# Attention in pairs of heads: scores in the two row halves of TensorE's array, values in its two column halves

## The chip, the cores and the metric

The kernel runs on one core of a Trainium2 chip. The metric is the time of one execution in microseconds (us), measured on the device. Lower is better. The engines are TensorE (PE in the rows, its weight loads PEld), VectorE (DVE), ScalarE (ACT), GpSimd (POOL) and SyncE (SP), whose queue issues most transfers.

## What is computed

One decoder layer over 256 tokens of width 1024. The change touches two parts of its first sub-layer: causal attention with 8 heads of 64 (one block of 256 keys, so every head is plain causal softmax with a distance bias), and a gated linear recurrence (HGRN2) with 4 heads of 128, in chunks of 64 tokens. Cut from the reference:

```
s_own = (jnp.einsum('bhqd,bhkd->bhqk', qc, k_own).astype(F32)
         - slopes[None, :, None, None] * dist_own[None, None])
s_own = jnp.where(dist_own[None, None] >= 0, s_own, -jnp.inf)
...
probs = jax.nn.softmax(scores, axis=-1).astype(v.dtype)
...
a = jnp.einsum('bhntd,bhnsd->bhnts', qh * jnp.exp(b - b_ref), kh * jnp.exp(b_ref - b))
ds = jnp.einsum('bhnsd,bhnsv->nbhdv', kh * jnp.exp(b_last - b), vh)
...
mixed = (jax.nn.sigmoid(ga) * (ya @ w_branch_a[l])
         + jax.nn.sigmoid(gb) * (yb @ w_branch_b[l]))
```

Behind it come the output projection, a layer norm, and the PEER part: 16384 experts, all of which are multiplied densely, in a U stage and a V stage that take most of the time.

## The kernel before

All large weights run through PE in pieces of 128x1024 in a ring of four (`raw`, `w_hi`, `w_lo`): SP loads piece m into `raw` when the low part of piece m-4 is made, ACT copies it to `w_hi`, DVE makes `w_lo` (`split_lo`, L1318), and PE multiplies high and low parts in three matmuls (L931 to L933). Two pieces make a block b; the blocks 8 to 33 hold the input projections, branch projections, output projection and query projection. Every block is 48 matmuls of 256 columns. Each engine has one program written out by hand in order of the blocks, and each step waits for semaphores.

Attention and HGRN are fp32 and lie between the blocks. On PE they are in `after(b)`, behind block b. A head h passes through it in four blocks: its products (L1101, L1102: queries of rows 0 to 127 with 128 keys, then queries 128 to 255 with 256 keys, both with 64 contracted rows into bank `px[0]`) behind block 11+h; DVE adds the distance bias and takes the maximum (L1402 to L1406) at the head of its block 13+h, ahead of the two `split_lo` of that block; ACT takes the exponentials (L754), DVE normalises (L1475 to L1477); three transposes (L1110, into `px[1]`) behind block 12+h; ACT copies them to `pT` in its block 14+h; values (L1119, L1120, into one 64-row half of bank `px[2]`) behind block 13+h. One half of the array in rows or in columns is used at a time. DVE and ACT run up to two blocks ahead of PE, so that their "block 13+h" lies beside PE's block 11+h or 12+h.

HGRN's steps are in the same function: `aT` in block 12, the transposes of `k_l` in 13, the state matmuls (L1078) in 14 and 15, the outputs (L1089, L1092) in 17, the transposes of `o_nat` (L1131) in 19. They use three banks: `pv[0]`, `pv[1]`, `px[3]`.

Of the kernel before, what the change touches and what calls it, by code (L numbers as in the profile page):

```python
# [5 lines left out]
P = 128  # L6
# [4 lines left out]
ALU = mybir.AluOpType  # L11
# [3 lines left out]
T = 256  # L15
# [3 lines left out]
HEADS = 8  # L19
# [89 lines left out]
def layer(nc, xT_d, x_d, c_d, ada1_d, ada3_d, w_ada_d, b_cols_d, b_ada_d, w1_d, ws_d, lb_d, norm_g_d, ln1_g_d, ln1_b_d, ln1_cols_d,  # L109
          keys_d, u_d, v_d, u_rows_d, ln2_g_d, ln2_b_d, x1_d, gates_d, out_d):  # L110
    with ExitStack() as ctx:
# [88 lines left out]
        pT = sb("pT", AR + 16640, [3 * P])  # L200
# [185 lines left out]
        def _(sp):  # L386
# [52 lines left out]
            for b in range(FIRST + 2, NA):  # L439
# [3 lines left out]
                if b == BRANCH + 2:  # L443
                    sp.wait_ge(pv_done, HEADS)
# [182 lines left out]
        def _(act):  # L627
# [67 lines left out]
            for b in range(FIRST + 2, NA):  # L695
# [33 lines left out]
                if b == 14:  # L729

                    for t, src in enumerate((px[3], pv[0])):
# [8 lines left out]
                if b == 15:  # L740
                    for t, src in enumerate((pv[1], px[3])):
                        act.wait_ge(kl_done, t + 1)
                        copy(kl_nat[:, t], src[:, :].rearrange("p (h t) -> p h t", h=HG)).then_inc(kl_ready, 1)
                if b == 19:
                    for t, src in enumerate((px[3], pv[0])):
# [30 lines left out]
                if b == 21:  # L776

                    for t, src in enumerate((pv[1], px[3])):
# [148 lines left out]
        def _(pe):  # L927
# [122 lines left out]
            def after(b):  # L1050

                if b == 12:
                    pe.wait_ge(qk_ready, 1)
                    pe.wait_ge(act_took, evac_count(QA + 1))
                    for t, dst in enumerate((px[3], pv[0])):
# [25 lines left out]
                if b == 17:  # L1081
                    pe.wait_ge(aT_ready, 1)
                    pe.wait_ge(state_ready, 3)
                    for t, dst in enumerate((px[3], pv[0])):
# [10 lines left out]
                h = b - 11  # L1095
                if 0 <= h < HEADS:
                    pe.wait_ge(act_took, evac_count(KA + 1))
                    if h >= 1:
                        pe.wait_ge(s_max, h)
                    r = slice((h % 2) * DH, (h % 2 + 1) * DH)  # L1100
                    nc.tensor.matmul(px[0][:, 0:P], qT[r, h // 2, 0:P], kT[r, h // 2, 0:P], start=True, stop=True)  # L1101
                    nc.tensor.matmul(px[0][:, P:3 * P], qT[r, h // 2, P:T], kT[r, h // 2, :], start=True, stop=True) \  # L1102
                        .then_inc(s_done, 1)

                def transposes(h):
                    pe.wait_ge(p_ready, h + 1)
                    if h >= 1:
                        pe.wait_ge(pT_ready, h)
# [859 lines left out]
```

## Time and profile before

| | |
|---|---|
| median of 3 runs | 984.92 us (984.75 to 985.06) |
| the profiled execution, its time | 984.99 us |
| its span (first to last instruction) | 983.2 us |
| mean granted clock of TensorE | 0.997 of 2.4 GHz |
| PE busy | 967.6 us, 98% |
| DVE, ACT, POOL busy | 794.3, 511.9, 373.7 us |
| transfers over the span | 239.56 MB, mean 244 GB/s |

Attention and HGRN lie between 83.7 and 163.5 us. In rows of the timeline the columns are the start in us, the duration in us, engine, line, operation, output and inputs, shape, and how many of the same kind were merged. Ends of matmuls are modelled, so the distance between starts tells what one costs. "128*64" is the part of the array that is used, rows by columns. A matmul in fp32 leaves two records, a transpose one.

### The profile page before, as it was taken

What the parts mean: (1) busy time and instruction counts of PE and PEld (TensorE: products, weight loads), DVE (VectorE), ACT (ScalarE), POOL (GpSimd) and SP (SyncE); (2) the same over time, 40 slices, a digit from 0 to 9 for tenths busy, and PEclk for the clock granted to TensorE, in tenths of its full rate; (3) what the DMA queues carried; (4) which work ended last, traced back from release to release, by engine and by line L of the source; (5) the groups of instructions that cost most, each with busy time, mean ns of one, the idle gap of its engine ahead of it and who ended that gap; (6) DMA issues with size and microseconds to landing.
All of it is one profiled execution on the core that took longest, in us unless ns stands there. A gap on an engine that the chain in (4) does not pass through costs nothing.

```text
span 983.2 us, 17773 instructions
## 1 busy us (share of the span) xinstructions
PE 967.6 (98%) x6823; PEld 894.3 (91%) x6823; DVE 794.3 (81%) x1538; ACT 511.9 (52%) x737; POOL 373.7 (38%) x234
## 2 busy tenths in 40 slices
PE   8999999999999999999999999999999999999996
PEld 8999889999999999999999999888888888888884
DVE  6979888894887989887688888787875878987866
ACT  5477656655445464546444444544445444445542
POOL 1010101001888787777887774122231222100002
PEclk9999999999999999999999999999999999999998
DMA  9987958985656787886766666788879989986661
GB/s 354 412 301 278 335 164 303 326 259 215 194 193 180 195 205 173 218 198 184 175 166 158 151 172 200 253 300 290 301 266 387 311 304 329 339 286 221 214 193 43
DMA packets 86659, 239.56 MB, mean 244 GB/s; under 512 B 26928, under 2 KB 27952, under 8 KB 84912
## 3 DMA queue, kind: packets, MB, share of 16 engines
q1 hardware_dynamic: 59536, 207.94, 62.3%
q0 software_dynamic: 26752, 30.49, 13.5%
q8 instruction: 54, 0.88, 0.4%
q14 instruction: 29, 0.24, 0.1%
q10 hardware_dynamic: 288, 0.01, 0.0%
HBM read 227.84 MB, written 10.55 MB: 242 GB/s over the span
## 4 chain that ended last, share of the span: by engine, by line
PE 91%; DVE 4%; DMA 2%; ACT 1%; SPq 1%; POOL 1%; issue 0%; POOLq 0%; ACTq 0%; DVEq 0%
PE px L1256 35%; PE pw L931 16%; PE pw L932 16%; PE pw L933 15%; PE px L1231 3%; DMA raw<-in_w 2%; DVE w_lo L1318 1%; PE pv L933 1%; PE pv L932 1%; PE pv L931 1%; PE px L931 1%; PE px L932 1%; PE px L933 1%; PE px L1188 0%; PE px L1119 0%
## 5 line engine op out<-in xcount | busy, mean ns | idle before, releaser
L629 ACT ACTIVATE w_hi<-raw 128x1024 fp32r<-128x1024 f32 x308 | 324.8, 1058 | 295.7 <-PE px L1256 157.9
L1318 DVE TENSOR_TENSOR w_lo<-raw,w_hi 128x1024 fp32r<-128x1024 f32 x285 | 347.2, 1226 | 96.3 <-ACT w_hi L629 94.8
L931 PE MATMUL pw<-a_hi,w_hi 128*128 128x240 f32 (+1 forms) x1248 | 348.1, 279 | 0.3 <-DVE a_lo L1568 0.3
L932 PE MATMUL pw<-a_lo,w_hi 128*128 128x240 f32 (+1 forms) x1248 | 344.2, 276 | 0.0
L933 PE MATMUL pw<-a_hi,w_lo 128*128 128x240 f32 (+1 forms) x1248 | 344.2, 276 | 0.0
L582 POOL DMA_INDIRECT gates_spill<-gate,place x128 | 231.9, 1812 | 65.9 <-issue 44.0
L931 PEld LDWEIGHTS pw<-a_hi,w_hi 128*128 128x128 f32 x1248 | 236.4, 189 | 2.3 <-issue 1.2
L932 PEld LDWEIGHTS pw<-a_lo,w_hi 128*128 128x128 f32 x1248 | 236.4, 189 | 0.0
L933 PEld LDWEIGHTS pw<-a_hi,w_lo 128*128 128x128 f32 x1248 | 236.4, 189 | 0.0
L1256 PE MATMUL px<-w_hi,ws_lo 128*128 128x512 f32 x512 | 159.0, 389 | 0.0
L1256 PE MATMUL px<-w_lo,ws_hi 128*128 128x512 f32 x512 | 158.9, 389 | 0.0
L1256 PE MATMUL px<-w_hi,ws_hi 128*128 128x512 f32 x512 | 158.8, 389 | 0.0
L1256 PEld LDWEIGHTS px<-w_hi,ws_lo 128*128 128x128 f32 x512 | 96.1, 188 | 20.0
L1256 PEld LDWEIGHTS px<-w_lo,ws_hi 128*128 128x128 f32 x512 | 96.1, 188 | 19.9
L1256 PEld LDWEIGHTS px<-w_hi,ws_hi 128*128 128x128 f32 x512 | 96.1, 188 | 19.8
L881 ACT ACTIVATE W<-pw 128x480 f32<-128x480 f32 (+11 forms) x64 | 34.3, 536 | 99.2 <-PE pw L933 99.1
L587 POOL DMA_INDIRECT sp_row<-in_v,sp_idx x16 | 28.6, 1790 | 99.3 <-DVE sp_acc L1851 81.2
L545 POOL DMA_DIRECT2D gates_spill<-zero x16 | 11.8, 737 | 140.2 <-DVE w_lo L1318 140.2
L587 POOL DMA_INDIRECT sp_row<-in_u_rows,sp_idx x16 | 28.4, 1776 | 90.7 <-DVE sp_w L1837 86.5
L512 POOL TENSOR_TENSOR w_lo<-raw,w_hi 128x1024 fp32r<-128x1024 f32 x22 | 52.4, 2403 | 20.9 <-ACT w_hi L629 20.9
L1799 DVE TENSOR_TENSOR ws_lo<-W,ws_hi 128x240 fp32r<-128x240 f32 x128 | 51.2, 402 | 0.0
L629 ACT ACTIVATE ws_hi<-W 128x240 fp32r<-128x240 f32 x128 | 49.3, 387 | 1.2 <-DVE W L1792 1.2
(382 smaller groups left out, 1239.3 us busy)
## 6 DMA issues: line engine op xcount, KB each, us to landing
raw<-in_u SPq DMA_DIRECT2D x128, 512.0 KB, 4.3
raw<-in_v SPq DMA_DIRECT2D x128, 512.0 KB, 4.3
raw<-in_ws SPq DMA_DIRECT2D x52, 512.0 KB, 6.7
ada<-in_ada SPq DMA_DIRECT2D x20, 512.0 KB, 6.9
ada<-in_w_ada SPq DMA_DIRECT2D x16, 512.0 KB, 7.4
gates_spill<-zero POOLq DMA_DIRECT2D x16, 512.0 KB, 7.6
g_row<-gates_spill SPq DMA_DIRECT2D x32, 256.0 KB, 5.1
raw<-in_w SPq DMA_DIRECT2D x7, 1024.0 KB, 11.8
```

The costliest lines, as they stand in the source:

```text
L512: nc.gpsimd.tensor_tensor(w_lo[:, m % RING], raw[:, m % RING], w_hi[:, m % RING].bitcast(F32), ALU.subtract) \
L582: nc.gpsimd.indirect_dma_start(gates_d, bass.IndirectOffsetOnAxis(ap=place[:, h, k:k + 1], axis=0), gate[0][:, h, k:k + 1], None, compute_ ...
L587: nc.gpsimd.indirect_dma_start(sp_row[x % 2][:, :], None, table, bass.IndirectOffsetOnAxis(ap=sp_idx[:, x % NS:x % NS + 1], axis=0)).then_ ...
L629: return nc.scalar.activation(out, in_, ACT.Copy, **kw)
L881: last = nc.scalar.activation(W[:, 2 * g:2 * g + 2, 0:left], src[:, :, 0:left], ACT.Gelu)
L931: nc.tensor.matmul(out, lh, rh, start=start and x == 0, stop=False)
L932: nc.tensor.matmul(out, lh, rl, start=False, stop=False)
L933: last = nc.tensor.matmul(out, ll, rh, start=False, stop=stop and x == len(pairs) - 1)
L1231: last = nc.tensor.matmul(px[n % 4][:, y * P:(y + 1) * P], oh_i[n % 2][:, y], oh_j[n % 2][:, y], start=True, stop=True)
L1256: last = nc.tensor.matmul(px[2 * t + half][:, :], l[:, v % RING, q], r[:, half * 512:(half + 1) * 512], start=v == 0 and x == 0, stop=v == ...
L1318: v.tensor_tensor(w_lo[:, m % RING], raw[:, m % RING], w_hi[:, m % RING].bitcast(F32), ALU.subtract).then_inc(lo_ready, 1)
L1799: v.tensor_tensor(ws_lo[:, r % RING, 0:TD], W[:, r], ws_hi[:, r % RING, 0:TD].bitcast(F32), ALU.subtract).then_inc(wsplit_lo, 1)
```

## The change

Heads go in pairs j = 0 to 3. Products: the two heads of a pair alternate between the row halves of the array and write to `px[0]` and `px[1]`. Transposes: six, into `px[2]` and `px[3]`. Values: three rounds of 128 columns, in each of which the two heads alternate between the column halves, written into the last quarter of `px[2]` and `px[3]`. Products and the transposes of the pair before stand behind the odd blocks 11 to 19, values behind the even blocks 14 to 20. DVE and ACT treat a pair at once, in odd blocks; DVE's bias and maximum of pair j now wait for the transposes of pair j-1. HGRN gives up `px[3]` and uses `pv[0]` and `pv[1]`; the state matmuls of chunks 0 and 1 stand behind block 14 and those of chunk 2 behind block 15, where they wait for DVE's first copy of the state.

```diff
         prob = sb("prob", AR + 15872, [2, 3 * P])
-        pT = sb("pT", AR + 16640, [3 * P])
+        pT = sb("pT", AR + 16640, [2, 3 * P])
...
-    h = b - 13
-    if 0 <= h < HEADS:
-        act.wait_ge(s_max, h + 1)
-        x = h % 2
-        for t, q in enumerate((slice(0, P), slice(P, 3 * P))):
-            last = nc.scalar.activation(prob[:, x, q], prob[:, x, q], ACT.Exp,
-                                        bias=rmax[:, 2 * x + t:2 * x + t + 1],
-                                        accum_out=rsum[:, 2 * x + t:2 * x + t + 1])
+    j = (b - 13) // 2
+    if b % 2 and 0 <= j < HEADS // 2:
+        act.wait_ge(s_max, j + 1)
+        for x in range(2):
+            for t, q in enumerate((slice(0, P), slice(P, 3 * P))):
+                last = nc.scalar.activation(prob[:, x, q], prob[:, x, q], ACT.Exp,
+                                            bias=rmax[:, 2 * x + t:2 * x + t + 1],
+                                            accum_out=rsum[:, 2 * x + t:2 * x + t + 1])
         last.then_inc(p_exp, 1)
-    h = b - 14
-    if 0 <= h < HEADS:
-        act.wait_ge(pT_done, h + 1)
-        if h >= 1:
-            act.wait_ge(pv_done, h)
-        copy(pT[:, :], px[1][:, 0:3 * P]).then_inc(pT_ready, 1)
+    j = (b - 15) // 2
+    if b % 2 and 0 <= j < HEADS // 2:
+        act.wait_ge(pT_done, j + 1)
+        if j >= 1:
+            act.wait_ge(pv_done, j)
+        for x in range(2):
+            last = copy(pT[:, x], px[2 + x][:, 0:3 * P])
+        last.then_inc(pT_ready, 1)
...
-    for h in range(1, HEADS, 2):
-        if b == h + 15:
-            act.wait_ge(pv_done, h + 1)
-            copy(yaT[:, h // 2], px[2][:, 0:T]).then_inc(ya_copied, 1)
+    j = (b - 16) // 2
+    if b % 2 == 0 and 0 <= j < HEADS // 2:
+        act.wait_ge(pv_done, j + 1)
+        for t in range(TT):
+            last = copy(yaT[:, j, t * P:(t + 1) * P], px[2 + t][:, 3 * P:4 * P])
+        last.then_inc(ya_copied, 1)
...
     if b == 13:
         pe.wait_ge(qk_ready, 2)
-        for t, dst in enumerate((pv[1], px[3])):
-            if t:
-                pe.wait_ge(aT_copied, 1)
+        for t, dst in enumerate((pv[1], pv[0])):
+            pe.wait_ge(aT_copied, t + 1)
...
     if b in (14, 15):
-        for n in ((0,) if b == 14 else (1, 2)):
-            dst = (pv[0], pv[1], px[3])[n]
-            pe.wait_ge(kl_ready, n // 2 + 1)
-            pe.wait_ge(aT_copied, 2)
-            if n:
-                pe.wait_ge(kl_ready, 2)
+        for n in ((0, 1) if b == 14 else (2,)):
+            dst = pv[n % 2]
+            pe.wait_ge(kl_ready, 2)
+            if n == 2:
+                pe.wait_ge(state_ready, 1)
             t, q = n // 2, slice((n % 2) * CH, (n % 2 + 1) * CH)
             for h in range(HG):
...
-    h = b - 11
-    if 0 <= h < HEADS:
+    def products(j):
         pe.wait_ge(act_took, evac_count(KA + 1))
-        if h >= 1:
-            pe.wait_ge(s_max, h)
-        r = slice((h % 2) * DH, (h % 2 + 1) * DH)
-        nc.tensor.matmul(px[0][:, 0:P], qT[r, h // 2, 0:P], kT[r, h // 2, 0:P], start=True, stop=True)
-        nc.tensor.matmul(px[0][:, P:3 * P], qT[r, h // 2, P:T], kT[r, h // 2, :], start=True, stop=True) \
-            .then_inc(s_done, 1)
...
-    def transposes(h):
-        pe.wait_ge(p_ready, h + 1)
-        if h >= 1:
-            pe.wait_ge(pT_ready, h)
-        for x in range(3):
-            last = nc.tensor.transpose(px[1][:, x * P:(x + 1) * P], prob[:, h % 2, x * P:(x + 1) * P], ident[:, :])
+        if j >= 1:
+            pe.wait_ge(s_max, j)
+        for q, k, o in ((slice(0, P), slice(0, P), slice(0, P)), (slice(P, T), slice(0, T), slice(P, 3 * P))):
+            for x in range(2):
+                r = slice(x * DH, (x + 1) * DH)
+                last = nc.tensor.matmul(px[x][:, o], qT[r, j, q], kT[r, j, k], start=True, stop=True)
+        last.then_inc(s_done, 1)
...
+    def transposes(j):
+        pe.wait_ge(p_ready, j + 1)
+        if j >= 1:
+            pe.wait_ge(pT_ready, j)
+            pe.wait_ge(ya_copied, j)
+        for x in range(2):
+            for y in range(3):
+                q = slice(y * P, (y + 1) * P)
+                last = nc.tensor.transpose(px[2 + x][:, q], prob[:, x, q], ident[:, :])
         last.then_inc(pT_done, 1)
-    def values(h):
-        pe.wait_ge(pT_ready, h + 1)
+    def values(j):
+        pe.wait_ge(pT_ready, j + 1)
         pe.wait_ge(act_took, evac_count(VA + 1))
-        if h >= 2 and h % 2 == 0:
-            pe.wait_ge(ya_copied, h // 2)
-        o, v = slice((h % 2) * DH, (h % 2 + 1) * DH), slice(h * DH, (h + 1) * DH)
-        nc.tensor.matmul(px[2][o, 0:T], va[:, 0, v], pT[:, 0:T], start=True, stop=False)
-        nc.tensor.matmul(px[2][o, P:T], va[:, 1, v], pT[:, T:3 * P], start=False, stop=True).then_inc(pv_done, 1)
...
-    if 0 <= b - 12 < HEADS:
-        transposes(b - 12)
-    if 0 <= b - 13 < HEADS:
-        values(b - 13)
+        for t, a, y in ((0, 0, 0), (1, 0, 1), (1, 1, 2)):
+            for x in range(2):
+                v = slice((2 * j + x) * DH, (2 * j + x + 1) * DH)
+                last = nc.tensor.matmul(px[2 + t][x * DH:(x + 1) * DH, 3 * P:4 * P], va[:, a, v],
+                                        pT[:, x, y * P:(y + 1) * P], start=a == 0, stop=a == t)
+        last.then_inc(pv_done, 1)
...
+    j = (b - 11) // 2
+    if b % 2 and 0 <= j < HEADS // 2:
+        products(j)
+    if b % 2 and 1 <= j <= HEADS // 2:
+        transposes(j - 1)
+    j = (b - 14) // 2
+    if b % 2 == 0 and 0 <= j < HEADS // 2:
+        values(j)
...
-    h = b - 13
-    if 0 <= h < HEADS:
-        x = h % 2
-        dve.wait_ge(s_done, h + 1)
-        if h == 0:
+    j = (b - 13) // 2
+    if b % 2 and 0 <= j < HEADS // 2:
+        dve.wait_ge(s_done, j + 1)
+        if j == 0:
             dve.wait_ge(consts, 3)
-        if h >= 2:
-            dve.wait_ge(pT_done, h - 1)
-        link(v.scalar_tensor_tensor(prob[:, x], dist[:, :], -(2.0 ** (-8.0 * (h + 1) / HEADS)), px[0][:, 0:3 * P],
-                                    ALU.mult, ALU.add))
-        v.reduce_max(rmax[:, 2 * x:2 * x + 1], prob[:, x, 0:P], AX)
-        link(v.reduce_max(rmax[:, 2 * x + 1:2 * x + 2], prob[:, x, P:3 * P], AX))
-        mark(v.tensor_scalar(rmax[:, 2 * x:2 * x + 2], rmax[:, 2 * x:2 * x + 2], -1.0, None, ALU.mult), s_max, h + 1)
+        else:
+            dve.wait_ge(pT_done, j)
+        for x in range(2):
+            ins = v.scalar_tensor_tensor(prob[:, x], dist[:, :], -(2.0 ** (-8.0 * (2 * j + x + 1) / HEADS)),
+                                         px[x][:, 0:3 * P], ALU.mult, ALU.add)
+        link(ins)
+        top = rmax[:, 0:4].rearrange("p (x t) -> p x t", t=2)
+        v.reduce_max(top[:, :, 0], prob[:, :, 0:P], AX)
+        link(v.reduce_max(top[:, :, 1], prob[:, :, P:3 * P], AX))
+        mark(v.tensor_scalar(rmax[:, 0:4], rmax[:, 0:4], -1.0, None, ALU.mult), s_max, j + 1)
...
-    h = b - 13
...
-        dve.wait_ge(p_exp, h + 1)
-        link(v.reciprocal(rinv[:, 2 * x:2 * x + 2], rsum[:, 2 * x:2 * x + 2]))
-        v.tensor_scalar(prob[:, x, 0:P], prob[:, x, 0:P], rinv[:, 2 * x:2 * x + 1], None, ALU.mult)
-        v.tensor_scalar(prob[:, x, P:3 * P], prob[:, x, P:3 * P], rinv[:, 2 * x + 1:2 * x + 2], None,
-                        ALU.mult).then_inc(p_ready, 1)
+    j = (b - 13) // 2
+    if b % 2 and 0 <= j < HEADS // 2:
+        dve.wait_ge(p_exp, j + 1)
+        link(v.reciprocal(rinv[:, 0:4], rsum[:, 0:4]))
+        for x in range(2):
+            for t, q in enumerate((slice(0, P), slice(P, 3 * P))):
+                ins = v.tensor_scalar(prob[:, x, q], prob[:, x, q], rinv[:, 2 * x + t:2 * x + t + 1], None, ALU.mult)
+        ins.then_inc(p_ready, 1)
```

PE, in the order of the program, all that stands between block 15 and block 16 and between block 16 and block 17 (the rows of the blocks themselves, L931 to L933, lie between the `px2` row with `pT` and the next `px0` row). Before:

```order
L1078 MATMUL pv<-vh_113,kl_nat_106 128x128 [waits kl_ready,aT_copied]
L1078 MATMUL pv<-vh_113,kl_nat_106 128x128 x3
L1078 MATMUL px3<-vh_113,kl_nat_106 128x128 [waits kl_ready,aT_copied]
L1078 MATMUL px3<-vh_113,kl_nat_106 128x128 x3
L1101 MATMUL px0<-kT_118,qT_117 128x128 [waits s_max,act_took]
L1102 MATMUL px0<-kT_118,qT_117 128x256
L1110 MATMUL px1<-ident_54,prob_120 128x128 [waits pT_ready,p_ready]
L1110 MATMUL px1<-ident_54,prob_120 128x128 x2
L1119 MATMUL px2<-pT_121,va_119 64x256 [waits ya_copied,act_took,pT_ready]
L1120 MATMUL px2<-pT_121,va_119 64x128
```

Behind block 16 stood the same without the four rows of L1078. After the change, behind block 15:

```order
L1080 MATMUL pv<-vh_113,kl_nat_106 128x128 [waits state_ready,kl_ready]
L1080 MATMUL pv<-vh_113,kl_nat_106 128x128 x3
L1104 MATMUL px0<-kT_118,qT_117 128x128 [waits s_max,act_took]
L1104 MATMUL px1<-kT_118,qT_117 128x128
L1104 MATMUL px0<-kT_118,qT_117 128x256
L1104 MATMUL px1<-kT_118,qT_117 128x256
L1115 MATMUL px2<-ident_54,prob_120 128x128 [waits ya_copied,pT_ready,p_ready]
L1115 MATMUL px2<-ident_54,prob_120 128x128 x2
L1115 MATMUL px3<-ident_54,prob_120 128x128 x3
L1124 MATMUL px2<-pT_121,va_119 64x128 [waits act_took,pT_ready]
L1124 MATMUL px2<-pT_121,va_119 64x128
L1124 MATMUL px3<-pT_121,va_119 64x128 x4
```

The last three rows stand behind block 16, where nothing else is left. Products and transposes are gone from there, and the second head's products have moved up into the row half beside the first head's.

DVE at its block 17, the head of the block to the normalising. Before:

```order
L1402 SCALAR_TENSOR_TENSOR prob_120<-dist_122,px0 128x384 [waits pT_done,s_done]
L1404 TENSOR_REDUCE rmax_72<-prob_120 128x1 [waits dve_chain]
L1405 TENSOR_REDUCE rmax_72<-prob_120 128x1
L1406 TENSOR_SCALAR rmax_72<-rmax_72 128x2 [waits dve_chain]
L1318 TENSOR_TENSOR w_lo_51<-raw_49,w_hi_50 128x1024 [waits hi_ready,s_max]
L1318 TENSOR_TENSOR w_lo_51<-raw_49,w_hi_50 128x1024 [waits hi_ready]
L1459 TENSOR_TENSOR state_116<-state_116,decay_71 128x512 [waits ds_done]
```

After the change:

```order
L1412 SCALAR_TENSOR_TENSOR prob_120<-dist_122,px0 128x384 [waits pT_done,s_done]
L1412 SCALAR_TENSOR_TENSOR prob_120<-dist_122,px1 128x384
L1416 TENSOR_REDUCE rmax_72<-prob_120 128x2 [waits dve_chain]
L1417 TENSOR_REDUCE rmax_72<-prob_120 128x2
L1418 TENSOR_SCALAR rmax_72<-rmax_72 128x4 [waits dve_chain]
L1328 TENSOR_TENSOR w_lo_51<-raw_49,w_hi_50 128x1024 [waits hi_ready,s_max]
L1328 TENSOR_TENSOR w_lo_51<-raw_49,w_hi_50 128x1024 [waits hi_ready]
L1471 TENSOR_TENSOR state_116<-state_116,decay_71 128x512 [waits ds_done]
```

The first row's wait for `pT_done` was for the transposes of two heads back, and is for those of the pair just before now; the two `w_lo` rows stand behind twice the work. In block 18 the first five rows are missing on DVE.

## Rows read from the trace of the kernel before

**Rows 1.** Page, part 1: busy us, share of the span, instructions of each engine.

```profile
PE 967.6 (98%) x6823; PEld 894.3 (91%) x6823; DVE 794.3 (81%) x1538; ACT 511.9 (52%) x737; POOL 373.7 (38%) x234
```

**Rows 2.** Waits of PE from 60 to 175 us: total, times, longest.

```profile
PE px L1110 <- DVE prob L1477: 0.2, 1, 0.2
```

**Rows 3.** Windows: length, busy by engine, clock, share of transfer engines, GB/s.

```profile
80.00:100.00 20.00, 20.00 (x162) 19.08 (x162) 19.72 (x29) 14.78 (x26) 1.42 (x2) 1.00 0.90 315
...
165.00:180.00 15.00, 15.00 (x127) 15.00 (x126) 13.29 (x17) 10.48 (x10) 1.50 (x2) 1.00 1.03 408
200.00:210.00 10.00, 10.00 (x86) 10.00 (x85) 9.83 (x16) 5.08 (x6) 0.71 (x1) 1.00 0.81 281
```

**Rows 4.** Timeline of PE behind block 13: products, transposes, values, dense again.

```profile
100.39 0.49 PE L1101 MATMUL px<-kT,qT 64*128 64x128 f32 x2
...
101.24 0.55 PE L1110 MATMUL px<-ident,prob 128*128 128x128 f32 x3
101.72 0.65 PE L1119 MATMUL px<-pT,va 128*64 128x256 f32 x2
...
102.51 0.39 PE L931 MATMUL pw<-a_hi,w_hi 128*128 128x256 f32 x1
```

**Rows 5.** Timeline of PE behind block 12: transposes, then dense.

```profile
93.29 0.55 PE L1110 MATMUL px<-ident,prob 128*128 128x128 f32 x3
93.60 0.36 PE L931 MATMUL pw<-w_hi,a_hi 128*128 128x256 f32 x1
```

**Rows 6.** Timeline of PE, block 20: first and last matmul, then block 21's first.

```profile
156.79 0.36 PE L931 MATMUL pw<-a_hi,w_hi 128*128 128x256 f32 x1
...
162.51 0.28 PE L933 MATMUL pw<-a_hi,w_lo 128*128 128x256 f32 x1
...
163.51 0.39 PE L931 MATMUL pw<-a_hi,w_hi 128*128 128x256 f32 x1
```

**Rows 7.** PE at the PEER scores: timeline, and the window of L1188 alone.

```profile
247.34 1.16 PE L1188 MATMUL px<-keys,qpT 64*128 64x128 f32 x16
248.43 0.38 PE L931 MATMUL pw<-a_hi,w_hi 128*128 128x240 f32 x1
...
247.30:247.36 0.06, 0.02 (x2) 1.00 0.83 341
```

**Rows 8.** Timeline of PE in HGRN's outputs, two of seven like steps.

```profile
136.44 0.44 PE L1089 MATMUL pv<-vh,aT 128*64 128x128 f32 x4
136.66 0.44 PE L1092 MATMUL pv<-state,q_x 128*64 128x128 f32 x4
```

**Rows 9.** Timeline of PE behind block 15: 16 records of L1078, then the products.

```profile
117.07 0.82 PE L1078 MATMUL pv<-vh,kl_nat 64*128 64x128 f32 x5
...
118.61 0.27 PE L1101 MATMUL px<-kT,qT 64*128 64x128 f32 x1
```

**Rows 10.** Timeline of DVE in its blocks 19 and 20.

```profile
139.24 0.56 DVE L1402 SCALAR_TENSOR_TENSOR prob<-dist,px 128x384 f32<-128x384 f32 x1 [3.23 <-PE px L1102]
...
140.68 2.36 DVE L1318 TENSOR_TENSOR w_lo<-raw,w_hi 128x1024 fp32r<-128x1024 f32 x2
...
145.61 0.16 DVE L1475 RECIPROCAL rinv<-rsum 128x2 f32<-128x2 f32 x1
...
146.27 0.20 DVE L1484 RECIPROCAL rms_i<-rms 128x8 f32<-128x8 f32 x1
...
150.16 0.55 DVE L1402 SCALAR_TENSOR_TENSOR prob<-dist,px 128x384 f32<-128x384 f32 x1
...
151.59 2.36 DVE L1318 TENSOR_TENSOR w_lo<-raw,w_hi 128x1024 fp32r<-128x1024 f32 x2
```

**Rows 11.** Timeline of ACT for one head: exponentials, then two copies.

```profile
130.46 0.40 ACT L754 ACTIVATE prob<-prob,rmax 128x128 f32<-128x128 f32 x1 [2.19 <-DVE rmax L1406]
...
131.36 0.47 ACT L629 ACTIVATE pT<-px 128x384 f32<-128x384 f32 x1
131.73 0.37 ACT L629 ACTIVATE yaT<-px 128x256 f32<-128x256 f32 x1
```

More of the change, by code:

```diff
@@ L443, in _ @@
                 if b == BRANCH + 2:
-                    sp.wait_ge(pv_done, HEADS)
+                    sp.wait_ge(pv_done, HEADS // 2)
                     sp.dma_start(x_nat[:, :, :], x_d.rearrange("(a p) n -> p a n", p=P)).then_inc(x_landed, 16)
@@ L729, in _ @@
                 if b == 14:
-                    for t, src in enumerate((px[3], pv[0])):
+                    for t, src in enumerate((pv[1], pv[0])):
                         act.wait_ge(aT_done, t + 1)
@@ L740, in _ @@
                 if b == 15:
-                    for t, src in enumerate((pv[1], px[3])):
+                    for t, src in enumerate((pv[1], pv[0])):
                         act.wait_ge(kl_done, t + 1)
@@ L744, in _ @@
                 if b == 19:
-                    for t, src in enumerate((px[3], pv[0])):
+                    for t, src in enumerate((pv[1], pv[0])):
                         act.wait_ge(o_done, t + 1)
                         copy(o_nat[:, t], src[:, :]).then_inc(o_copied, 1)
-                h = b - 13
-                if 0 <= h < HEADS:
-                    act.wait_ge(s_max, h + 1)
-                    x = h % 2
-                    for t, q in enumerate((slice(0, P), slice(P, 3 * P))):
-                        last = nc.scalar.activation(prob[:, x, q], prob[:, x, q], ACT.Exp,
-                                                    bias=rmax[:, 2 * x + t:2 * x + t + 1],
-                                                    accum_out=rsum[:, 2 * x + t:2 * x + t + 1])
-                    last.then_inc(p_exp, 1)
-                h = b - 14
-                if 0 <= h < HEADS:
-                    act.wait_ge(pT_done, h + 1)
-                    if h >= 1:
-                        act.wait_ge(pv_done, h)
-                    copy(pT[:, :], px[1][:, 0:3 * P]).then_inc(pT_ready, 1)
+                j = (b - 13) // 2
[6 more added lines that the diff above has]
+                                                        accum_out=rsum[:, 2 * x + t:2 * x + t + 1])
+                    last.then_inc(p_exp, 1)
+                j = (b - 15) // 2
[6 more added lines that the diff above has]
+                    last.then_inc(pT_ready, 1)
                 if b == 19:
@@ L776, in _ @@
                 if b == 21:
-                    for t, src in enumerate((pv[1], px[3])):
+                    for t, src in enumerate((pv[1], pv[0])):
                         act.wait_ge(ybT_done, t + 1)
@@ L1054, in after @@
                     pe.wait_ge(act_took, evac_count(QA + 1))
-                    for t, dst in enumerate((px[3], pv[0])):
+                    for t, dst in enumerate((pv[1], pv[0])):
                         for h in range(HG):
@@ L1061, in after @@
                     pe.wait_ge(qk_ready, 2)
-                    for t, dst in enumerate((pv[1], px[3])):
-                        if t:
-                            pe.wait_ge(aT_copied, 1)
+                    for t, dst in enumerate((pv[1], pv[0])):
+                        pe.wait_ge(aT_copied, t + 1)
                         for h in range(HG):
@@ L1083, in after @@
                     pe.wait_ge(state_ready, 3)
-                    for t, dst in enumerate((px[3], pv[0])):
+                    for t, dst in enumerate((pv[1], pv[0])):
                         for h in range(HG):
@@ L1126, in after @@
+                    last.then_inc(pv_done, 1)
[7 more added lines that the diff above has]
+                    values(j)
                 if b == 19:
                     pe.wait_ge(yb_ready, 1)
-                    for t, dst in enumerate((pv[1], px[3])):
+                    for t, dst in enumerate((pv[1], pv[0])):
@@ L1135, in after @@
                     pe.wait_ge(gt1_ready, 2)
-                    pe.wait_ge(pT_ready, HEADS)
+                    pe.wait_ge(pT_ready, HEADS // 2)
                     for half in range(2):
@@ L1453, in _ @@
                         dve.wait_ge(ds_done, n + 1)
-                        src = (pv[0], pv[1], px[3])[n]
+                        src = pv[n % 2]
                         if n == 0:
@@ L1491, in _ @@
                     dve.wait_ge(act_hi, 1)
-                    for t, src in enumerate((pv[1], px[3])):
+                    for t, src in enumerate((pv[1], pv[0])):
                         q = slice(t * P, (t + 1) * P)
```

2 lines of the change are left out of this document (removed).

## The prediction

> **What bounds the kernel now.** I read the page's busy times first: TensorE (PE) is busy for 967.6 us of the 983.2 us span [rows 1]. Then the waits of PE between 60 and 175 us, the stretch in which this code runs: one wait, 0.2 us [rows 2]. So every matmul taken out of this stretch moves all that follows, as long as VectorE (DVE), ScalarE (ACT) and the transfers still deliver before PE asks. That condition is not empty: DVE is busy for 19.72 of the 20 us from 80 to 100, and for 9.83 of 10 from 200 to 210; the transfers fill 1.03 of their engines from 165 to 180 [rows 3]. The reader is to see two things: a PE without holes, and a DVE that is nearly as full.
>
> Then PE's timeline after weight block 13, for the price of each step of a head by the distance between starts [rows 4]: products 0.85 (100.39 to 101.24), three transposes 0.48 when values follow, values 0.79 (101.72 to 102.51). Where dense work follows the transposes, they take 0.31 [rows 5]. A whole block is 5.72 from its first to its last matmul, and values alone put 1.00 between the last matmul and the next dense one, where 0.12 would stand without them: net 0.88 [rows 6].
>
> **The change part by part.**
>
> *Attention on PE.* Now: 8 products, 6.80; transposes seven times 0.48 and once 0.31, 3.67; values seven times 0.79 and once 0.88, 6.41. Sum 16.88.
>
> Afterwards four pairs. Do two heads in the two row halves run at once? The profile of before has that pattern: the PEER scores L1188 alternate row halves and banks. Their 16 records take 1.09 from the first to the next dense matmul, and two of them start in the first 0.06 us [rows 7]. One half alone needs 0.11 for a record, so 16 in a row would take 1.76 and two streams of eight 0.88; 1.09 is two streams and 0.2 for the change of shape, which the 0.85 of one head contains as well. A pair of products is thus 0.85. For the column halves the HGRN outputs L1089 and L1092 serve: alternating halves of one bank, four records in 0.22 (136.44 to 136.66), 0.055 each [rows 8]. The values of a pair are 12 records of 128 columns, 0.66, the same as the two records of 256 and two of 128 that one head costs now; so 0.79, or 0.88 alone in a block. Transposes: no overlap, six take 0.31 and three more at 0.11, 0.64.
>
> Sum: products 3.40; transposes 2.56; values three times alone, 2.64, and once behind state matmuls, 0.79 and up to 0.15 for changing from row to column halves, 0.94. Together 9.54. Taken out: 7.3.
>
> *Smaller items.* The one wait of PE, 0.2, stands before head 7's transposes; their normalised probabilities are ready a block earlier now: gain 0.2. HGRN's 28 output matmuls and 16 transposes only change banks: nothing. The state matmuls: where one set follows another in the other row half they overlap at the seam, 16 records in 1.54 instead of 1.76 [rows 9]. Before there are two such seams (n=0 against head 3's products, n=1 against n=2), afterwards one: loss 0.2. From aT to dense no shape changes in block 12 any more: gain 0.1. So 7.3 + 0.2 - 0.2 + 0.1 = 7.4.
>
> *ACT and DVE.* The work shrinks: three Exp/Sigmoid/Sqrt table loads fewer on ACT, some fixed costs on DVE. What counts is that it comes in lumps, in odd blocks only, and that DVE has a new wait at the head of the lump: pT_done(j), the transposes of the pair before (until now one head back in the other half of `prob`, long done). Behind it in DVE's queue stand the two w_lo splits of the block, on which PE and SP's next loads of raw wait. The lump's size: one head's maximum takes 1.43 (150.16 to 151.59) [rows 10]. Two take at most 2.86; merged, with two drains fewer, I take 2.3.
>
> Two places decide. D is the first dense matmul after the transposes of the pair before.
>
> (a) Values in blocks 16 and 18 need pT. The last transpose ends 0.2 after D (93.29 + 0.55 against 93.60) [rows 5]: DVE starts at D + 0.2, ends at D + 2.5 (at most 3.1); ACT's exponentials take 0.90 a head (130.46 to 131.36), 1.80 for two; the copies 0.37 and 0.47 [rows 11]. pT at D + 5.1, at most 5.7. PE asks at 5.72 + 0.12, D + 5.85. No wait, with 0.15 to 0.7 in hand. The two splits behind the maximum are ready by D + 5.5, the first is wanted at D + 6.7.
>
> (b) Block 19, counted from the first matmul D of block 18. DVE: maximum until D + 2.5; splits, squares and their sum as now, 140.68 to 145.61, 4.93; normalising 0.66 a head (145.61 to 146.27), 1.1 to 1.3 for two; the norm chain 146.27 to 150.16, 3.89. So `o_nat` at D + 12.6, by the upper ends 13.4. PE wants it at 5.85 + 0.88 + 5.85 + 0.64 = D + 13.2. Then PE needs w_lo for block 20 another 0.9 later, DVE delivers it 1.2 later: D + 13.8 (14.6) against 14.1. The cover is 0.3 here; gone, it costs up to 0.5. Now DVE is 5 us ahead at this point (split at 151.59, used at 156.79). After block 20 the lead comes back, since a block has no maximum any more.
>
> Against the profiled execution's own 984.99 the sum gives 977.6; the median of the runs shown lies 0.07 lower: **977.5 us**.
>
> A rule speaks against the full overlap. What the trace shows: two score records, one of each half, start within the first 0.06 us, although the first matmul leaves two records of 0.11 each [rows 7]. The Trainium skill, "TensorE: Matmul & The Clock Gate", Part 3, has matmuls start and end strictly in the order of the program. Held against single records, that rule would give the second of the rivals below, 978.8 instead of 977.5; the trace, with the second head starting before the first one's second record, speaks for 977.5.
>
> **The rivals.**
>
> *As summed* (977.5; own range 976.6 to 978.3): 0.66.
>
> *First: DVE comes onto the path* in blocks 15 to 20: the lump and its wait leave PE one or two holes of 0.5 to 2 us. For it: the cover of 0.3 at (b), the full DVE [rows 3]. Against: DVE idled 3.23 us before the maximum at 139.24 [rows 10], and DVE's work becomes less. 978.3 to 981: 0.18.
>
> *Second: records in strict order*: the second half starts a matmul only when the first half has started the second record of its own. A record of 256 columns is 0.22, one of 128 is 0.11: a pair of products costs 0.22 more, the values 0.11, four of each 1.3. 978.8, with 0.04; against it stand the two starts at 247.34 [rows 7].
>
> *Third: the halves don't overlap* for these shapes: 6 records of 0.11, 0.66 more for each of 8 groups, 5.3; 982.8. Against it stand the scores and the outputs [rows 7, 8]: 0.03.
>
> *Fourth: given back later*: PE arrives 7.4 earlier in the stretch where transfers are full and DVE has 9.83 of 10 [rows 3], and waits there until the old time: 984.9. Against: loads and splits are released by PE and by the splits themselves, so they move with it. 0.05, with parts of it in the range above.
>
> *Fifth: slower.* The pT chain (a) is longer than thought. It stands before the values of blocks 16 and 18, so each us beyond 5.85 costs two. It eats the gain from 5.85 + 3.7 = 9.5 us on, and 987 is reached at 10.6, where I have 5.1 to 5.7. The other end of the price of a maximum doesn't reach that. 0.04.
>
> **How the numbers follow.** 0.2% of this kernel, 1.97 us, is about what a measurement can tell from no change: faster is below 982.95. The likeliest case and the first three rivals fall below it: 0.91. Same 0.05, slower 0.04. The range of 8 in 10 takes the likeliest case and most of the first rival: 976.2 to 979.9.
>
> **What would show it.** PE's timeline: four groups L1104 of 8 records with about 0.85 to the next step; four of L1124 with 12 records and net 0.88 in blocks 16, 18 and 20; block 12 followed by aT alone; the first matmul of block 21 at 156.1 instead of 163.5. No wait of PE for pT (ACT) before L1124, nor for `o_nat` or w_lo at block 20: a row there of a few tenths is the first rival, several us the fifth. If L1104 takes 1.5, the halves don't overlap; 1.07 is strict order. If block 21 comes on time but the end doesn't, the stretch from 165 to 220 gave it back. The prediction is wrong if that stretch holds more than 1 us of new waits, or if raw pieces land late there.

## The result: 980.3 us, and the profile after

The changed kernel takes 980.33 us (median of 6 runs, 979.66 to 980.7), the kernel before 985.11 beside it (984.75 to 986.45): ratio 0.9949, interval 0.9936 to 0.9962. It is faster by 4.8 us; 7.6 were predicted, and 980.33 lies outside the range (976.2 to 979.9). The profiled execution took 979.66 us, its span is 977.9, 5.3 shorter than before.

Where the attention runs, the profile shows what was worked out. Page part 1 (PE's busy time, 967.6 before [rows 1]), then PE's timeline behind block 13 and around blocks 20 and 21 (start, duration of the group):

```profile
PE 959.3 (98%) x6839; PEld 890.4 (91%) x6839; DVE 791.8 (81%) x1522; ACT 507.6 (52%) x738; POOL 375.0 (38%) x234
```

```profile
98.90 0.93 PE L1104 MATMUL px<-kT,qT 64*128 64x128 f32 x8
99.76 0.88 PE L1115 MATMUL px<-ident,prob 128*128 128x128 f32 x6
100.39 0.36 PE L935 MATMUL pw<-a_hi,w_hi 128*128 128x256 f32 x1
...
154.85 0.88 PE L1124 MATMUL px<-pT,va 128*64 128x128 f32 x12
155.66 0.39 PE L935 MATMUL pw<-a_hi,w_hi 128*128 128x256 f32 x1
```

A pair's products take 0.86 between starts, six transposes 0.63, a pair's values 0.81. Block 21 begins at 155.66; before it was 163.51 [rows 6]. 0.17 of the 7.85 was there before the first products, so the attention gives 7.7 on PE. No wait of PE stands between 60 and 175 us.

Behind that, 2.4 of the 7.7 are lost again by the profiles, 2.9 by the medians. In the rows, m_lo is the low part of the gated sum of the two branches (`mix`), x the normalised rows in the layer norm, br_a and br_b the two gated branches. Waits of PE from 175 to 222 us, and of ACT for raw pieces from 140 on (total, times, longest; the kernel before has 0.4, once, from 150 on in the second row):

```profile
PE pw L935 <- DVE m_lo L1524: 1.7, 1, 1.7
PE px L1008 <- ACT x L821: 1.4, 1, 1.4
```

```profile
ACT w_hi L629 <- DMA raw<-in_ws: 8.0, 6, 3.1
```

PE's wait for m_lo is new, the wait for ACT's x was 1.0 before: 2.1 more in these two. The first dense matmul behind the layer norm starts at 220.25 against 225.57, 5.3 sooner, and so does everything behind it. ACT's timeline has the pieces that matter, 30, 31 and 34 (the other three waits are 2.1 in sum).

```profile
161.11 1.06 ACT L629 ACTIVATE w_hi<-raw 128x1024 fp32r<-128x1024 f32 x1 [3.12 <-DMA raw<-in_ws]
163.44 1.06 ACT L629 ACTIVATE w_hi<-raw 128x1024 fp32r<-128x1024 f32 x1 [1.26 <-DMA raw<-in_ws]
...
166.29 1.92 ACT L793 ACTIVATE sig_a<-sig_a 128x2048 f32<-128x2048 f32 x1
...
175.82 1.06 ACT L629 ACTIVATE w_hi<-raw 128x1024 fp32r<-128x1024 f32 x1 [1.56 <-DMA raw<-in_ws]
```

Behind the late pieces stand the gates' sigmoids: 166.29, that is 10.6 behind block 21's start; before 172.48, 9.0 behind it. DVE's first gated branch waits for them. First after, then before:

```profile
170.04 0.69 DVE L1425 TENSOR_TENSOR br_a<-pw,sig_a 128x512 f32<-128x512 f32 x1 [1.91 <-ACT sig_b L793]
```

```profile
176.23 0.69 DVE L1413 TENSOR_TENSOR br_a<-pw,sig_a 128x512 f32<-128x512 f32 x1 [1.38 <-ACT sig_b L789]
```

That is 6.2 sooner where block 21 was 7.85 sooner: 1.7 are gone. From there DVE works nearly without a gap up to the last m_lo, and loses 0.8 more at piece 34 (idle before its split at 176.92); the last m_lo comes at 190.39 against 195.70, 5.3 sooner. So DVE's chain hands both losses on, and PE's end follows it.

Why the pieces are late, two further views show. DVE's timeline:

```profile
135.24 1.02 DVE L1412 SCALAR_TENSOR_TENSOR prob<-dist,px 128x384 f32<-128x384 f32 x2 [2.26 <-PE px L1115]
...
147.50 2.35 DVE L1328 TENSOR_TENSOR w_lo<-raw,w_hi 128x1024 fp32r<-128x1024 f32 x2
```

SyncE's queue, first after, then before: pieces 28 and 29, two ada tiles (512 KB each of the matrix `w_ada`, which DVE sums up between the splits), pieces 30 and 31:

```profile
148.75 1.46 SPq L393 DMA_DIRECT2D raw<-in_ws  x2
150.63 0.80 SPq L423 DMA_DIRECT2D ada<-in_ada  x2
152.16 1.46 SPq L393 DMA_DIRECT2D raw<-in_ws  x2
```

```profile
152.85 1.47 SPq L393 DMA_DIRECT2D raw<-in_ws  x2
154.73 0.80 SPq L423 DMA_DIRECT2D ada<-in_ada  x2
156.92 1.46 SPq L393 DMA_DIRECT2D raw<-in_ws  x2
```

The maximum in DVE's block 19 began at 139.24 before and at 135.24 now, 4.0 sooner, since DVE waits there for PE's work behind block 17. PE's products there began 4.9 sooner (133.40 against 138.28), but the maximum now waits for the six transposes behind them too, and that hands back 0.9. From there to the splits of block 20 DVE needs 12.3 us without a wait in both kernels (139.24 to 151.59 [rows 10], 135.24 to 147.50). So the splits and SyncE's issues behind them come 4.1 sooner, PE's block 21 comes 7.85 sooner. And from 148.75 to 160 us 7.5 MB are asked for: pieces 28 to 33, four ada tiles, x_nat and gt (1 MB of rows of x and 0.5 MB of a bias, both read ahead of the layer norm), and two of the clears (0.5 MB of zeros each, issued by GpSimd). Windows after (DMA share and GB/s at the end):

```profile
125.00:130.00 5.00, 5.00 (x45) 4.87 (x45) 4.96 (x11) 1.20 (x3) 0.15 (x1) 1.00 0.10 38
157.00:177.00 20.00, 20.00 (x169) 20.00 (x169) 16.79 (x20) 12.18 (x11) 3.88 (x3) 1.00 1.02 406
```

7.5 MB are 15 times 524,288 bytes; at 406 GB/s that is 19.4 us wherever the burst begins, an estimate and a lower bound: its first part, from 148.75 to 157, moved 255 GB/s. The Trainium skill, "Perfetto Trace Analysis", under "Roofline", puts one core's ceiling at its 16 DMA engines, about 435 GB/s; the trace agrees (406 over 20 us at a share of 1.02). Such a stretch has nothing in hand, though the same engines stand at 0.10 from 125 to 130. The pieces are not slower than before, only due sooner: piece 31 took 10.0 us from issue to landing before (158.1 to 168.1, and ACT took it at 169.62, when PE let it go) and 10.1 now (153.3 to 163.4, taken at once), 4.7 sooner where PE was 7.85 sooner; 1.55 of the difference of 3.2 had been in hand, so it comes 1.6 late.

### The profile page after: what moved, and what is told of

Same layout as the page of the kernel before. It is cut to its first block, busy times and chain, and to the rows that moved or that the text cites. A ratio compares the mean times of both kernels' runs of the same rounds, so it can differ in the third digit from the quotient of the medians.

```text
span 977.9 us, 17766 instructions
## 1 busy us (share of the span) xinstructions
PE 959.3 (98%) x6839; PEld 890.4 (91%) x6839; DVE 791.8 (81%) x1522; ACT 507.6 (52%) x738; POOL 375.0 (38%) x234
## 4 chain that ended last, share of the span: by engine, by line
PE 90%; DVE 4%; DMA 3%; ACT 1%; issue 1%; POOL 1%; SPq 0%; POOLq 0%; ACTq 0%; DVEq 0%
PE px L1266 35%; PE pw L935 16%; PE pw L936 15%; PE pw L937 15%; PE px L1241 3%; DMA raw<-in_ws 2%; DMA raw<-in_w 1%; DVE w_lo L1328 1%; PE px L936 1%; PE px L935 1%; PE px L937 1%; DVE ada L1337 0%; PE px L1198 0%; PE pv L937 0%; PE pv L936 0%
```

## The experiments

All were timed in five rounds beside the kernel before (985.15 to 985.20). Three theories at first: **full transfers** (the burst is more than its stretch holds), **late issue** (DVE's splits release the pieces too late), **chain** (DVE's and ACT's own chain through the branches sets the end).

### The burst 2 MB smaller, in both kernels

Of the four ada tiles of blocks 22 and 23 only one partition of 128 is loaded; DVE's sums over them work on old values, so these two kernels don't compute the whole function.

```
-                sp.dma_start(ada[:, t % ADA_SLOTS], src).then_inc(...)
+                rows = slice(0, 1) if t in ada_at(22) + ada_at(23) else slice(0, P)
+                sp.dma_start(ada[rows, t % ADA_SLOTS], src[rows]).then_inc(...)
```

> The changed kernel with only one partition (4 KB in place of 512 KB) of each of the four ada tiles of blocks 22 and 23 transferred; VectorE's sums over them stay and work on old values, so mod2 is not the reference's. 2 MB fewer in the burst that begins at 148.75 us. Full transfers: pieces 30 and 31 no longer queue behind the first two tiles (1 MB, 2.5 us) and pieces 32 on not behind four (5 us); ScalarE's waits of 3.12 and 1.26 us for pieces 30 and 31 go, the sigmoids of the gates start at about 164 in place of 166.29, the wait for piece 34 goes too, and most of the 2.5 us returns: 977.8 to 978.5 us. Late issue: issue times stay, so at most a third comes back, 979.5 us or more. Chain: the chain's length from the sigmoids on is unchanged; if it doesn't start sooner the time is 980.3.

> The kernel before with the same 2 MB left out (four ada tiles cut to one partition, mod2 not the reference's). There ScalarE waited only 0.4 us for raw pieces between 150 and 222 us. Full transfers: the kernel before paid for these 2 MB at most those 0.4 us, so 984.5 to 985.1 us, and the difference between this run and the changed kernel with the same cut is 7 us or more: the whole price of the attention. Chain or late issue: 984.9 too, but then the changed kernel with the cut stays at 979.5 or above and the difference stays near 5 us.

Measured, in the changed kernel: 977.25 us (977.12 to 979.31), and in the kernel before 985.22 (ratio to before 0.9999, 0.9990 to 1.0008). The same cut is worth 3.1 us in the changed kernel and nothing in the kernel before; between the two kernels with the cut lie 8.0 us. In the changed kernel ACT's waits for pieces fall from 8.0 to one, of piece 28:

```profile
ACT w_hi L630 <- DMA raw<-in_ws: 1.6, 1, 1.6
```

PE's wait for m_lo is gone. Full transfers holds: the tiles cost nothing as such, only where PE comes early for what stands behind them.

### The same bytes, at another time

ada22_first issues block 22's two ada tiles ahead of its pieces:

```
+                if b == BRANCH:
+                    for t in ada_at(b):
+                        load_ada(t)
                 load_block(b)
-                for t in ada_at(b):
+                for t in ada_at(b) if b != BRANCH else ():
                     load_ada(t)
```

> The changed kernel with SyncE issuing the two ada tiles of block 22 ahead of that block's pieces instead of behind them. They wait only for ada_done, long reached, so they are issued at about 140.8 us in place of 150.6 and travel in the stretch 140 to 148.75, where the transfers used 0.5 to 0.7 of their engines; the same bytes, 1 MB fewer in the burst that begins at 148.75. Full transfers: pieces 30 to 35 land 2.5 us sooner, ScalarE's waits of 3.12 and 1.26 us shrink to below 2 in sum, the sigmoids start near 164.3 and the end is 1.5 to 2.5 us sooner: 977.8 to 978.8 us. If the lateness of pieces 28 and 29 matters instead, they too come sooner or stay, no loss. If only the number of bytes per block counted and not when they go, 980.3.

Measured: 978.41 us (978.19 to 978.97), 1.9 won with nothing left out. The tiles went out at 140.78, ACT's waits for pieces 30 and 31 are gone, the one for 34 is 1.46.

early_both adds earlier clears:

```
-                    pool.wait_ge(lo_ready, 4 + 46 * n // ZERO_DMAS)
+                    pool.wait_ge(lo_ready, {7: 21, 8: 22, 9: 24}.get(n, 4 + 46 * n // ZERO_DMAS))
```

> As ada22_first, and GpSimd's clears 8 and 9 (0.5 MB each, issued at 152.43 and 157.04 us) released by the splits of pieces 21 and 23, so at about 130.6 and 140 us. 2 MB fewer in the burst, all of them still transferred. Full transfers: as ada_less, which had 2 MB less in all: 977.2 to 977.9 us, waits of ScalarE for raw pieces between 150 and 180 under 1 us in sum. If clears don't hinder the loads because they are writes: as ada22_first alone.

Measured: 979.36 us (979.14 to 980.76), a miss. PE got a hole at block 20:

```profile
PE pw L938 <- DVE w_lo L1331: 1.8, 1, 1.8
```

The transfers did not make it: ACT copied block 20's two pieces at 143.13 without a wait for them, and they were ready when DVE began to split them at 147.91. The split itself was slow, beside GpSimd:

```profile
147.91 4.53 DVE L1331 TENSOR_TENSOR w_lo<-raw,w_hi 128x1024 fp32r<-128x1024 f32 x2
```

```profile
147.23 2.99 POOL L562 TENSOR_TENSOR acc_lo<-acc,acc_hi 128x1024 fp32r<-128x1024 f32 x1 [5.91 <-ACT acc_hi L632]
```

The two splits took 2.35 in the changed kernel (147.50). GpSimd has `acc_lo` behind clear 9 in its program; with that clear moved from 157.04 to 140.62, `acc_lo` no longer waited for it and came from 157.70 to 147.23, onto the split PE needed next. The first split ended at 151.3, and the issues of pieces 28 on with it (151.33 against 148.75). 979.36 less 1.8 is 977.6, what was expected, and behind block 20 PE waits for no m_lo; but that the clears alone are worth this is not shown by a run. The premise in best_a's expectation below, that the early clear and tiles made PE wait for pieces, is wrong for the same reason; best_a leaves clear 9 where it was, and with it `acc_lo` (156.72).

late_x moves x_nat, ln_cols and gt from block 24 to 26 (`if b == BRANCH + 4:`).

> The changed kernel with x_nat, ln_cols and gt (1.5 MB) loaded behind the pieces of block 26 instead of block 24. Their first readers on VectorE come at 193.4 (gt) and 198.9 us (x_nat) in the changed kernel's profile, so the later load leaves room. Full transfers (the 2.5 us given back are lost because the transfers of 157 to 177 us are more than that stretch holds): pieces 34 and 35, which ScalarE waited 1.56 us for, land up to 1.5 MB / 0.41 MB per us = 3.7 us sooner, that wait goes, and 0.8 to 1.2 us come back: 979.2 to 979.6 us. Pieces 30 and 31 are issued ahead of x_nat, so their lateness stays, and with it the later sigmoids. Late issue (the pieces of blocks 22 and 23 are asked for too late): no change from the pieces before x_nat, 980.3 us. Chain (VectorE's and ScalarE's own chain through the branches is the bound whatever lands): 980.3 us.

Measured: 982.81 us (981.04 to 985.31), 2.5 slower, a miss for all three. What full transfers said of piece 34 came true: ACT's wait for it is gone (its copy starts at 175.46 with no wait). But SyncE issues the 1.5 MB at 176.49, in front of piece 38, which ACT then waits for:

```profile
188.57 1.06 ACT L629 ACTIVATE w_hi<-raw 128x1024 fp32r<-128x1024 f32 x1 [2.93 <-DMA raw<-in_ws]
```

PE's wait for m_lo grows from 1.7 to 3.3. Another 0.9 of PE, for y_lo, comes from piece 29 landing late (ACT waits 2.81 at 156.53), ahead of anything that was moved. That the landing of one stream varies between executions is a reading of this and of the spread of 4.3 us; no run isolates it.

### DVE's side

ada18 moves the sums of block 18 to 27 and 28 (`20: 1, 21: 1, 22: 2, 23: 2, 27: 2, 28: 2`).

> The changed kernel with the two ada tiles of block 18 moved to blocks 27 and 28 (one more each). VectorE has 2 x 1.15 = 2.3 us less ahead of block 19 and so reaches its splits for blocks 20 and 21 up to 2.3 us sooner, though VectorE idled 2.26 us at 135.24 for PE's transposes, so the gain there may be nearly nothing. Late issue: if the splits at 147.50 move up by x us, the burst starts x us sooner, and the end comes x us sooner up to 2.5 us. As the idle time at 135.24 suggests x near 0, the time is 980.3, and VectorE's two more tiles in blocks 27 and 28 (2.3 us) can cost up to 2.3 us, 980.3 to 982.6, since VectorE works there without a gap. Full transfers: the order of the burst is unchanged, but the tiles of later blocks come two further on, so the same 980.3 or above. Chain: 981.5 to 982.6, since the added work stands on it.

Measured: 983.37 us (983.03 to 984.91), slower by 3.0, beyond the upper end given. The pieces 28 and 29 went out from 148.94 on, so x is 0 as expected: time freed ahead of a wait is no lead. The tiles cost in blocks 27 and 28 as work of DVE (PE waits 2.0 for x) and as bytes (ACT waits 3.23 for a piece at 199.89). Not all of the 3.0 is theirs: PE also waits 0.9 for y_lo, behind a late piece 29, ahead of anything that was moved.

sq_first takes the squares of `o_nat` into DVE's idle 2.26 us:

```
             for b in range(FIRST, NA):
+                if b == 19:
+                    sq = qh[:, :].rearrange("p (a n) -> p a n", a=TT)
+                    for t in range(TT):
+                        dve.wait_ge(o_copied, t + 1)
+                        last = v.tensor_tensor(sq[:, t], o_nat[:, t], o_nat[:, t], ALU.mult)
+                    link(last)
                 j = (b - 13) // 2
```

> The changed kernel with one move: in block 19 VectorE takes the two squares of o_nat (0.65 us each) ahead of the last maximum instead of behind the block's splits. VectorE idled 2.26 us there until the transposes of the pair before (135.24), and o_nat is copied by 132.4 and 134.1, so the squares fit into the idle time. All that follows on VectorE up to the splits of block 20 comes 1.2 us sooner (147.50 to 146.3), and so do SyncE's issues of pieces 28 and 29, the start of the burst. Theory now (two parts: VectorE's chain from block 17's end to those splits is as long as before, 12.3 us, so the burst starts only 4.1 us sooner than in the kernel before while PE is 7.85 ahead; and the burst, 7.5 MB, takes the same time): pieces 30 to 35 and the end come 1.2 us sooner, 979.1 us. If the start of the burst plays no part: 980.3.

Measured: 979.78 us (979.17 to 979.9), 0.55 won of 1.2, with ranges that overlap. The issues came 1.0 sooner (147.75). In the profile piece 30 was no sooner for it (ACT at 161.96), and DVE's split at 156.65 ran beside GpSimd's acc_lo and took 3.64 in place of 1.23. The changed kernel has the same meeting on y_lo (3.25 in place of 1.21, at 158.02), so that explains some 0.4 at most (an estimate from the two lengths). So late issue has a share, by this run a small one and near the noise.

sig_only moves sig_a's sigmoid from ACT's block 23 to the end of its block 22.

> The changed kernel with ScalarE taking the sigmoid of sig_a at the end of block 22 instead of in block 23: it then lies at 157.9 to 161.1 us, in ScalarE's wait for piece 30, together with the table load, and after block 21's evacuation only sig_b's sigmoid is left before the first br_a: gates ready at about 167.0 in place of 170.0. Transfers are as in the changed kernel. Chain through the branches: if the start of that chain sets the end, up to 2.5 us come back: 978 us. Full transfers: pieces 32 to 35 land no sooner, and the wait for piece 34 (till 175.82) remains, so at most the part lost before it is won and lost again at that piece: 979.6 to 980.3 us.

Measured: 980.86 us (979.98 to 981.37): nothing won. In its profile, of the slowest execution, ACT waited longer for piece 34 instead, and PE 1.5 for br_b besides the 1.7 for m_lo:

```profile
177.54 1.06 ACT L629 ACTIVATE w_hi<-raw 128x1024 fp32r<-128x1024 f32 x1 [3.68 <-DMA raw<-in_ws]
```

The chain is not the bound while the pieces are late.

### All together, and the control

best_a: ada22_first, sq_first and clears 7 and 8 at the splits of pieces 20 and 21 (`{7: 21, 8: 22}`); nothing is left out. best_b: sig_only's move as well. before_moves has the two moves of transfers, not the squares.

> The changed kernel with three moves, nothing left out: the ada tiles of block 22 issued ahead of its pieces (978.4 us alone), the squares ahead of the maximum (expected 1.2), and clears 7 and 8 released by the splits of pieces 20 and 21, at about 129 to 131 us where the transfers used a tenth of their engines, instead of 140.2 and 152.4. Only one of the three 0.5 MB clears stays in the burst, and none is left at 140, where the early clear together with the early ada tiles made PE wait for pieces of block 20. Theory (end of the burst): 977.2 to 977.9 us, the price of the attention alone, and no wait of PE between 140 and 176. If the early clears hinder pieces 24 and 25, issued at 129.5, a hole of PE at about 142.

> As best_a, and the sigmoid of sig_a taken at the end of block 22. With the pieces on time the chain of the branches can start as soon as block 21 is evacuated and sig_b's sigmoid is done, 1.8 to 3 us before the changed kernel's. If that chain (VectorE without a gap from the first br_a to the layer norm) is then the next bound, 975.5 to 976.5 us; if PE is, as best_a. Alone, the same move gave nothing (980.9), since piece 34 landed no sooner.

> The kernel before with the two moves of transfers that fit it (ada tiles of block 22 ahead of its pieces, clears 7 and 8 earlier). It had hardly a wait for raw pieces in this stretch and lost nothing when 2 MB were left out (985.22), so by the theory 984.7 to 985.2 us: the moves are worth nothing without the shorter attention. If they gained 1 us or more here too, the gain of the kernels above would not be what the attention change had given back.

Measured: best_a 977.48 us (977.43 to 978.21), ratio 0.9925 (0.9911 to 0.9938); best_b 976.84 (976.62 to 977.39), ratio 0.9918 (0.9905 to 0.9932); the moves of transfers in the kernel before 985.10, ratio 0.9998 (0.9989 to 1.0008). In best_a no wait of PE is left before the layer norm's; from 140 to 222 us:

```profile
ACT w_hi L632 <- DMA raw<-in_ws: 2.6, 3, 1.4
PE px L1011 <- ACT x L824: 1.0, 1, 1.0
```

From 985.10 to 977.48 is 7.6, what the attention was summed to (up to 0.55 of it can be the squares' move, which the kernel before doesn't have). With the pieces on time the sigmoid's move is worth 0.6, less than the 1 to 2 expected. PE is the bound there, and only its wait at the layer norm shrinks, from 1.0 to 0.7. In the profiles best_b was 0.5 ahead of best_a by 140 us already, in front of the move, so the move itself may be worth no more than 0.3.

### The halves, one head after the other

```
-                    for q, k, o in ((slice(0, P), ...), (slice(P, T), ...)):
-                        for x in range(2):
+                    for x in range(2):
+                        for q, k, o in ((slice(0, P), ...), (slice(P, T), ...)):
```

and the same for the values.

> The changed kernel with the two heads of a pair one after the other on TensorE, in the products and in the values (same instructions, banks, lumps on VectorE and ScalarE; only the order in which PE issues them). If the halves overlap because neighbouring instructions go to different halves, a pair of products takes 0.66 us more than the 0.85 measured (1.51), a pair of values 0.66 more than 0.81 (1.47), eight groups 5.3 us: block 21 begins at about 160.9 in place of 155.66. If they also overlapped in this order, nothing changes there. The end: PE then arrives only 2.4 us ahead of the kernel before, and by the theory of full transfers hardly anything is given back: 982.4 to 983.0 us, 2 to 2.7 above the changed kernel although 5.3 us of matmul time were added. If what is given back were a fixed price of the change instead (VectorE's lumps), the time would be 985.6.

Measured: 981.48 us (980.75 to 982.4). PE's timeline, a pair of products and then a pair of values:

```profile
83.92 0.93 PE L1104 MATMUL px<-kT,qT 64*128 64x128 f32 x8
84.78 0.38 PE L935 MATMUL pw<-w_hi,a_hi 128*128 128x256 f32 x1
...
108.19 1.14 PE L1124 MATMUL px<-pT,va 128*64 128x128 f32 x12
109.27 0.39 PE L935 MATMUL pw<-a_hi,w_hi 128*128 128x256 f32 x1
```

Products 0.86, as when alternating; values 1.08 against 0.81, not 1.47. Four times 0.27 is 1.1, and the median moved by 1.15. The span of the profile moved by 2.3: 0.2 was there before the first products, and PE waited 0.4 for y_lo behind a late piece 29. Both expectations for the end fall with their premise, so the run does not tell how the loss grows with PE's lead.

## Why the prediction was wrong

- **The price on PE was right.** Products 0.86 for 0.85, transposes 0.63 for 0.64, values 0.81 (alone 1.02 to the next dense matmul, net 0.90, for 0.88). Block 21 came at 155.66 where 156.1 stood: 0.17 of that lay ahead of the attention, the rest is a gain of 7.7 for 7.4.
- **No hole in blocks 12 to 20, right.** DVE's maximum of a pair took 2.3 (86.39 to 88.69), as taken. At block 20 the split was ready at 148.7, PE began at 148.93: cover 0.2 for 0.3. The first rival did not occur in its blocks.
- **Strict order and halves that don't overlap, rightly put low.** The products overlap even where the program has one head after the other.
- **The number fits a rival by chance.** 980.3 lies in the first rival's 978.3 to 981, but that rival has its holes in blocks 15 to 20, and there are none.
- **The step that failed** is in (b) and in the fourth rival: "After block 20 the lead comes back", and "loads and splits are released by PE and by the splits themselves, so they move with it." DVE is tied to PE at the end of block 17 (0.9 later than before, by its new wait for the transposes) and then works 12.3 us without a wait. So of PE's 7.7 us, 3.7 are won by neither DVE nor the queue of loads. The lead of DVE's split over PE at block 20 fell from 5.2 to 1.4, and there the text stopped: "the cover is 0.3" was priced for PE alone, not for SyncE, which issues the next pieces behind that split.
- **The second half of the same step:** the 19.4 us burst behind it. The view was there (transfers 1.03 from 165 to 180 [rows 3]) and the rival too, but as all or nothing, 984.9 with 0.05, where its partial form came true: 7.7 on PE, 4.8 at the end. Shown by the four runs with and without the cut (3.1 against nothing), and by ada22_first, where the same bytes at another time give back 1.9. How the loss divides between the lead that DVE didn't win and the length of the burst is argued from the traces; sq_first alone touches the first, near the noise.
- **GpSimd's meeting with DVE is not the cause.** y_lo at 158.02 takes 2.0 longer beside acc_lo, but the kernel before has such a meeting too (a split of 2.88 at 163.98), and so have ada_less (3.25) and best_a (3.86), which have the whole gain.
- The text named what would refute it: raw pieces late between 165 and 220, over 1 us of new waits. Both are there (piece 34 at 175.82, 2.1 us).

## What to carry to other kernels

When matmul time is taken out of a bound engine, ask at which point each other engine last waits for it: what is won behind that point isn't won by that engine, nor by the loads it releases. A stretch where transfers are full has a length of its own, bytes over rate; count the bytes from its first issue and set its end against the new due times. If it comes short, move loads into the idle stretch ahead rather than behind, and look what else stands behind a moved request on its own engine: it comes sooner too, and can land beside work that is due.

## What the runs showed of the hardware

- Two K=64 products of one head followed by two of the other row half took 0.86 us, the same as when alternating (0.86); the values of two column halves, three and three, took 1.08 against 0.81. So PE lets the halves overlap some way across the order of the program; what bounds how far was not tried.
- A VectorE split of 128x1024 took 3.64 us in place of 1.23 where GpSimd subtracted a tile of the same size; the same happened to y_lo in the changed kernel, 3.25 us at 158.02. In both, and in early_both and the kernel before, VectorE's instruction ended 1.1 us after GpSimd's (GpSimd at 159.2, 160.2, 150.2 and 165.8; VectorE at 160.3, 161.3, 151.3 and 166.9): it cost about what was left of GpSimd's.
- The same piece, 29, issued with 28 from 148.8 to 148.9 on behind the same requests, was taken by ACT at 155.02 in the changed kernel, when PE let it go, and at 156.53 in late_x and 157.90 in ada18, when it landed.
